# Two transformer blocks on one core: adaptive-norm blocks moved out of the even attention, its bias added by VectorE, its constants awaited later

## The reference

```python
def adaln(cond, w, b):                       # six shifts, scales and gates per layer, from the condition
    m = jax.nn.silu(cond) @ w + b            # 1024 -> 6144
    return jnp.split(m[:, None, :], 6, axis=-1)

# layer 0, the even mixer: 8 heads of window attention with a sink, 8 of neighbourhood attention
s_loc = jnp.einsum('bnqgrd,bnkgd->bngrqk', qb, kb) * scale
s_loc = jnp.where(valid[None, :, None, None], s_loc, NEG_INF)          # window: a mask
p = jax.nn.softmax(jnp.concatenate([s_loc, s_ctx, s_sink], axis=-1), axis=-1)
...
s_loc = jnp.einsum('brqhd,brikhd->brhqik', qg, kg) * scale + bias[None]   # near: a learned bias
s_loc = jnp.where(col_ok[:, None, :], s_loc, NEG_INF)
p = jax.nn.softmax(jnp.concatenate([s_loc, s_ctx], axis=-1), axis=-1)
```

## Time and profile before

| | |
|---|---|
| runs | 1917.2, 1918.7, 1922.2 us; median 1918.7 |
| profiled execution | 1921.6 us, span 1919.7 us |
| mean granted TensorE clock | 0.963 |
| TensorE busy | 1783.1 us, 93% of the span |
| VectorE, ScalarE, GpSimd busy | 927.3, 631.1, 183.8 us |
| bytes moved | 253.9 MB, mean 132 GB/s |

### The profile page before, as it was taken

The page is one execution under the profiler, slowest core; times in us unless marked ns, Lnnn a source line. Parts: engine busy times, 40 slices in busy tenths (PEclk is TensorE's granted clock), DMA queues, the critical chain, the costliest instruction groups (busy, mean ns, idle before and its releaser), DMA issues.

```text
span 1919.7 us, 25440 instructions
## 1 busy us (share of the span) xinstructions
PE 1783.1 (93%) x10056; PEld 1342.9 (70%) x10056; DVE 927.3 (48%) x1639; ACT 631.1 (33%) x1183; POOL 183.8 (10%) x202
## 2 busy tenths in 40 slices
PE   4999999989999999898989999899889789989998
PEld 1444555458888887453679998566679679879997
DVE  2122655254343433355736664434569853545544
ACT  3111544132222232233625443313322144034443
POOL 1001000100000001033000001001149200000000
PEclk8999999989999999998999999799889989999999
DMA  9222998132222321222044443223110234334442
GB/s 378 76 88 88 385 367 345 44 131 88 88 88 93 122 93 58 76 83 88 1 173 175 177 176 137 84 108 123 51 71 1 88 132 176 116 148 176 162 152 83
DMA packets 20885, 253.88 MB, mean 132 GB/s; under 512 B 2208, under 2 KB 4512, under 8 KB 5024
## 3 DMA queue, kind: packets, MB, share of 16 engines
q1 hardware_dynamic: 17712, 242.44, 33.2%
q10 hardware_dynamic: 3056, 9.82, 1.4%
HBM read 251.20 MB, written 1.05 MB: 131 GB/s over the span
## 4 chain that ended last, share of the span: by engine, by line
PE 81%; DVE 6%; POOL 4%; ACT 3%; issue 3%; DMA 2%; DVEq 0%; POOLq 0%; SPq 0%; ACTq 0%
PE bank L489 26%; PE bank L515 13%; PE bank L516 13%; PE bank L517 13%; PE bank L573 3%; PE bank L647 3%; PE bank L675 2%; POOL slab L2042 2%; PE bank L660 2%; PE bank L904 2%; DVE w_lo L1538 1%; POOL slab L2028 1%; DMA weights<-in_ada 1%; PE bank L652 1%; ACT w_hi L1147 1%
## 5 line engine op out<-in xcount | busy, mean ns | idle before, releaser
L489 PE MATMUL bank<-slab,weights 128*128 128x256 f32 (+2 forms) x1456 | 450.9, 469 | 17.5 <-DMA consts<-in_c 10.1
L489 PEld LDWEIGHTS bank<-slab,weights 128*128 128x128 f32 (+1 forms) x1456 | 277.7, 192 | 184.1 <-issue 141.0
L1538 DVE TENSOR_TENSOR w_lo<-weights,w_hi 128x1024 fp32r<-128x1024 f32 (+1 forms) x220 | 264.4, 1212 | 95.6 <-ACT w_hi L1147 94.8
L515 PE MATMUL bank<-h_hi,w_hi 128*128 128x256 f32 (+1 forms) x864 | 278.3, 322 | 25.4 <-DVE h_lo L1559 15.1
L1147 ACT ACTIVATE w_hi<-weights 128x1024 fp32r<-128x1024 f32 (+1 forms) x220 | 228.5, 1047 | 214.2 <-PE bank L517 209.5
L516 PE MATMUL bank<-h_lo,w_hi 128*128 128x256 f32 (+1 forms) x864 | 277.0, 321 | 0.0
L517 PE MATMUL bank<-h_hi,w_lo 128*128 128x256 f32 (+1 forms) x864 | 275.5, 319 | 0.0
L515 PEld LDWEIGHTS bank<-h_hi,w_hi 128*128 128x128 f32 x864 | 166.0, 192 | 42.2 <-issue 29.5
L516 PE MATMUL bank<-mlp_hidden_lo,w_hi 128*128 128x512 f32 (+1 forms) x512 | 174.4, 341 | 0.0
L516 PEld LDWEIGHTS bank<-h_lo,w_hi 128*128 128x128 f32 x864 | 166.2, 192 | 11.3
L517 PEld LDWEIGHTS bank<-h_hi,w_lo 128*128 128x128 f32 x864 | 165.6, 192 | 12.0
(11 more groups left out here) (206 smaller groups left out, 2338.4 us busy)
## 6 DMA issues: line engine op xcount, KB each, us to landing
weights<-in_ada SPq DMA_DIRECT2D x36, 2048.0 KB, 8.6
weights<-in_mlp_up SPq DMA_DIRECT2D x16, 2048.0 KB, 8.3
weights<-in_mlp_down SPq DMA_DIRECT2D x16, 2048.0 KB, 8.4
weights<-in_ffn_in SPq DMA_DIRECT2D x11, 2048.0 KB, 7.5
weights<-in_in SPq DMA_DIRECT2D x8, 2048.0 KB, 8.4
weights<-in_gate SPq DMA_DIRECT2D x6, 2048.0 KB, 7.5
weights<-in_ffn_out SPq DMA_DIRECT2D x8, 1408.0 KB, 6.0
weights<-in_even_in SPq DMA_DIRECT2D x4, 2048.0 KB, 11.6
```

Of the source, the lines that this page charges most:

```text
L489: last = mm(b[rows, 0:width], lhsT(k), rhs(k), start=k == 0, stop=k == kc - 1)
L515: mm(b[:, 0:width], wh, hi(k), start=k == 0, stop=False)
L1538: V.tensor_tensor(split_part(w_lo, q), raw_part(q), split_part(w_hi, q).bitcast(F32), ALU.subtract)\
```

## The change

1. *The table of adaptive-norm blocks.* The even attention keeps 18 of its 25 blocks, in four steps of seven (`7 * j // 4`). The other seven go: one behind the norm `mix1`, one before the sums of squares of `cq`, one before `uq` item 3, one behind the rotation of `kr`, one before the value products, one after the second token tile of them, and one in the delta network before its fifth masked sum. A batch may now hold blocks of two layers; the batches end elsewhere, and fold 3 moves from the even attention to step 2 of the odd one.
2. *The bias.* TensorE no longer multiplies the identity by the bias in 32 units. VectorE takes the maximum over the 256 context columns, and one instruction adds the bias to the first 256 columns in the bank and takes the maximum of the result and of the first maximum. TensorE's wait for `near_ready` is gone.
3. *The constants.* TensorE waits for `c0_in` at item 4 of the first projection instead of before it.
4. *Ring slots.* Where a block now falls between the taking of a weight block and its end, the entry of that weight block is kept aside and set later.

```diff
@@ -398,12 +398,14 @@
         }
 
 
-        ADA_BATCHES = [(0, 0, 4), (0, 4, 12), (1, 0, 12), (2, 0, 5), (2, 5, 12)]
-        ADA_ORDER = [(batch, n, blk) for batch, (n, lo, hi) in enumerate(ADA_BATCHES) for blk in range(lo, hi)]
-        ADA_ENDS = [sum(hi - lo for _, lo, hi in ADA_BATCHES[:batch + 1]) for batch in range(len(ADA_BATCHES))]
-        ADA_START, ADA_ATT = 4, 25
-        ada_steps = [5 * j // 4 for j in range(ADA_ATT)]
-        ada_ended = {ada_steps[ADA_ENDS[batch] - ADA_START - 1]: batch for batch in (1, 2, 3)}
+        ADA_BATCHES = [[(0, 0, 4)], [(0, 4, 12)], [(1, 0, 10)], [(1, 10, 12), (2, 0, 6)], [(2, 6, 12)]]
+        ADA_ORDER = [(batch, n, blk) for batch, runs in enumerate(ADA_BATCHES)
+                     for n, lo, hi in runs for blk in range(lo, hi)]
+        ADA_SIZES = [sum(hi - lo for _, lo, hi in runs) for runs in ADA_BATCHES]
+        ADA_ENDS = [sum(ADA_SIZES[:batch + 1]) for batch in range(len(ADA_BATCHES))]
+        ADA_START, ADA_ATT = 4, 18
+        ada_steps = [7 * j // 4 for j in range(ADA_ATT)]
+        ada_ended = {"even": {ada_steps[ADA_ENDS[batch] - ADA_START - 1]: batch for batch in (1, 2)}, "odd": {0: 3}}
 
 
         def even_items():
@@ -560,18 +562,18 @@
             def ada_block():
 
                 batch, n, blk = ADA_ORDER[ada[0]]
-                _, lo, hi = ADA_BATCHES[batch]
-                row = SIDES * (blk - lo)
+                at = ada[0] - ADA_ENDS[batch] + ADA_SIZES[batch]
+                row = SIDES * at
                 w = take_block(f"ada{n}", blk)
                 if ada[0] == 0:
                     pe.wait_ge(sem("cond_ready"), 2)
-                if blk == lo and batch:
+                if at == 0 and batch:
                     pe.wait_ge(sem("ada_copied"), batch)
                 window = slice(ADA_WIDE - SIDES - row, 2 * ADA_WIDE - SIDES - row)
                 for k in range(DC):
                     strip = slice(k % 4 * ADA_WIDE, (k % 4 + 1) * ADA_WIDE)
                     ins = mm(banks[ADA_BANK][strip, :], cond[:, n // 2, k, window], w[:, k, :],
-                             start=blk == lo and k < 4, stop=blk == hi - 1 and k >= 4)
+                             start=at == 0 and k < 4, stop=at == ADA_SIZES[batch] - 1 and k >= 4)
                 ins.then_inc(sem("ada_used"), 1)
                 ada[0] += 1
                 stream[-1][2] = ("ada_used", ada[0])
@@ -644,12 +646,7 @@
                         tags = [(name, "s", 2 * p), (name, "s", 2 * p + 1)]
                         for u, t in zip(pair, tags):
                             b = open_group(t)
-                            ins = mm(b[:, 0:u["n"]], u["q"], u["k"], start=True, stop=u["bias"] is None)
-                            if u["bias"] is None:
-                                close(ins, t)
-                        for u, t in zip(pair, tags):
-                            if u["bias"] is not None:
-                                close(mm(bank(t)[:, 0:LAT], ident, u["bias"], start=False, stop=True), t)
+                            close(mm(b[:, 0:u["n"]], u["q"], u["k"], start=True, stop=True), t)
                     if lag <= p < n + lag:
                         for j in (2 * (p - lag), 2 * (p - lag) + 1):
                             u = units[j]
@@ -679,8 +676,8 @@
                                     ins.then_inc(sem(f"{name}_pv"), 1)
                     if name == "even" and p in ada_steps:
                         ada_block()
-                    if name == "even" and p - 2 in ada_ended:
-                        ada_fold(ada_ended[p - 2])
+                    if p - 2 in ada_ended[name]:
+                        ada_fold(ada_ended[name][p - 2])
 
             def h_ready(name):
                 return lambda k: pe.wait_ge(sem(f"{name}_h"), k + 1)
@@ -712,7 +709,6 @@
             for _ in range(ADA_START - 2):
                 ada_block()
             ada_fold(0)
-            pe.wait_ge(sem("c0_in"), 16)
             items = ITEMS["even"]
             for blk in range(3):
                 w = take_block("even_in", blk)
@@ -722,6 +718,8 @@
                             before=h_ready("mix0") if i == 0 else None)
                     if mi == 3:
                         release_block(("even", i))
+                    if i == 4:
+                        pe.wait_ge(sem("c0_in"), 16)
                     if i and i % 4 == 0:
                         means_of("even", i // 4 - 1)
                     if i % 4 == 1 and i > 4:
@@ -745,7 +743,6 @@
             release_block(("vb", 3))
             rope("even", 4)
             pe.wait_ge(sem("even_roped"), 5)
-            pe.wait_ge(sem("near_ready"), 1)
             for t in range(4):
                 drained(pe, ("va", t))
                 drained(pe, ("vb", t))
@@ -757,6 +754,7 @@
 
 
             norm("mix1", TOK)
+            ada_block()
             pe.wait_ge(sem("c1_in"), 16)
             w = take_block("odd_in", 0)
             for i in range(3):
@@ -766,6 +764,8 @@
             release_block(("ckv", 0))
             w = take_block("odd_in_b", 0)
             product(("ckv", 1), DC, lambda k: w[:, k, 0:P], lambda k: h[:, k, :])
+            in_b = stream[-1]
+            ada_block()
             for name, n, width in (("cq", 3, LAT), ("ckv", 2, TOK)):
                 t = (name, "ss")
                 b = open_group(t, which=n)
@@ -776,17 +776,20 @@
                         ins.then_inc(sem(f"{name}_used"), 1)
                 close(ins, t)
             product(("kr", 0), DC, lambda k: w[:, k, P:P + 32], lambda k: h[:, k, :], rows=slice(64, 96))
-            release_block(("kr", 0))
+            in_b[2] = ("kr", 0)
             mean_of("kr", 0)
             pe.wait_ge(sem("cq_scaled"), 3)
             for blk in range(2):
                 w = take_block("uq", blk)
+                entry = stream[-1]
                 for hi in range(8):
                     i = blk * 8 + hi
+                    if i == 3:
+                        ada_block()
                     product(("uq", i), 3, lambda k: w[:, k, hi * MLA_QK:(hi + 1) * MLA_QK], lambda k: cq[:, k, :],
                             rows=slice(0, MLA_QK), width=LAT)
                     if hi == 7:
-                        release_block(("uq", i))
+                        entry[2] = ("uq", i)
                     if i and i % 4 == 0:
                         means_of("uq", i // 4 - 1)
                     if i >= 7 and i % 4 == 3:
@@ -814,15 +818,19 @@
             rope("uq", 15)
             release_block(("uk", 7))
             w = take_block("ukv", 1)
+            entry = stream[-1]
+            ada_block()
             for t in range(4):
                 for half in range(2):
                     product(("uv", 2 * t + half), 2, lambda k: ckv[:, k, t * P:(t + 1) * P],
                             lambda k: w[:, k, half * 512:(half + 1) * 512])
                 if t == 0:
                     means_of("uk", 1)
+                if t == 1:
+                    ada_block()
                 if t >= 2:
                     spread_of("uk", 1, 2 * (t - 2), 2)
-            release_block(("uv", 7))
+            entry[2] = ("uv", 7)
             pe.wait_ge(sem("uq_roped"), MLA_HEADS)
             pe.wait_ge(sem("uk_scaled"), 8)
             pe.wait_ge(sem("kr_copied"), MLA_HEADS)
@@ -928,6 +936,8 @@
                         heads(("qk", t), lambda hd: kT[:, hd, t * P:(t + 1) * P],
                               lambda hd: qT[:, hd, t * P:(t + 1) * P], which=1)
                 branch(*((6, "sx") if n < 4 else (4, "sb")), n % 4)
+                if n == 3:
+                    ada_block()
             tokens_first("kt", kT, "k_unit")
             for li in range(len(LEVELS)):
                 for t in range(4):
@@ -1190,8 +1200,8 @@
                 lag = a["lag"]
                 nprob, nprobT = len(a["prob"]), len(a["probT"])
                 for i in range(n + lag + 1):
-                    if name == "even" and i % 2 == 0 and i // 2 - 1 in ada_ended:
-                        ada_copy(ada_ended[i // 2 - 1])
+                    if i % 2 == 0 and i // 2 - 1 in ada_ended[name]:
+                        ada_copy(ada_ended[name][i // 2 - 1])
                     if i < n:
                         u = units[i]
                         t = (name, "s", i)
@@ -1404,14 +1414,17 @@
 
             def ada_bias(batch):
 
-                n, lo, hi = ADA_BATCHES[batch]
                 t = ("adaT", batch)
                 filled(dve, t)
-                got = bank(t)[:, 0:4 * ADA_WIDE].rearrange("p (m b s) -> p b m s", m=4, s=SIDES)[:, 0:hi - lo, :, :]
-                at = slice(4 * lo, 4 * hi)
-                V.tensor_tensor(mod[n][:, at, :].rearrange("p (b m) s -> p b m s", m=4), got,
-                                par(f"ada_b{n}").rearrange("p (b m s) -> p b m s", m=4, s=SIDES)[:, lo:hi, :, :], ALU.add)\
-                    .then_inc(free(t), 1)
+                got = bank(t)[:, 0:4 * ADA_WIDE].rearrange("p (m b s) -> p b m s", m=4, s=SIDES)
+                at = 0
```

(24 more changed lines are left out.)

## The result

The changed kernel takes **1910.2 us** (median of 6 runs, 1905.9 to 1912.3) against 1920.5 us for the kernel before in the same rounds (6 runs, 1917.2 to 1922.2): a ratio of 0.9945, 95% interval 0.9929 to 0.9961. It is faster, by 10.3 us. I had forecast 1897 us and a range that ended at 1906: half of the forecast gain is missing. A second measurement of the same kernel, beside a median of 1919.9 us for the kernel before, gave 1908.7 us (0.9938, 0.9918 to 0.9958).

The account below looks back on a forecast made before the run. TensorE was taken as the bound nearly everywhere. The terms -8.2 - 17.0 - 14.0 + 6.5 + 10.9 = -21.8 us gave 1899.8 us for the profiled execution, 1897 us as median; range 1888 to 1906 us.

Parts of the forecast that it names:

- part 4: Even attention: TensorE waits for VectorE in steps without a block and in heads with sinks, +6.5 us (+3 to +14).
- Part 1: Start: even constants awaited at item 4, first product at 34.14 us instead of 42.37, -8.2 us.
- Rival E: Start: bound otherwise, the even constants not the last to come, so little gained there; 1905 us, chance 0.03.
- Part 2: Even attention: bias by VectorE takes 17.0 us off TensorE; VectorE pays +0.25 us a unit (+0.15 to +0.55).
- rival A: Even attention: VectorE's adding instruction costs double, +0.55 us a unit; time 1904 to 1905 us, chance 0.12.
- Part 2 and 3: Even attention: TensorE loses 16 pairs of bias products, -17.0 us, and seven blocks and one fold, -14.0 us.
- Rival C: Even attention: the clock falls after waits of 1.5 to 1.8 us, three falls of 1.7 us; 1902 us, chance 0.1.
- Part 5: Six blocks to odd projections, one to delta network, a fold to odd attention: +10.9 us, including +5.2 at uq item 3.
- Rival B: Odd projections: the ring starves the scattered blocks, each later one waiting for its load; +10 us, 1907 us, chance 0.06.
- Rival D: Even attention: VectorE becomes the bound if the adding instruction takes some 1.6 us; about 1931 us at 1.8, chance 0.03.

Follow-up runs that it names:

- aligned: The changed kernel with the same 18 even-attention blocks put in the 16 steps that carry a bias, and steps 2 and 30: 1894.1 us (0.9856).
- after_again: The changed kernel itself, unchanged, measured again in later rounds: 1908.7 us (0.9938).
- blocks_only: The kernel before with only the new list of blocks; bias still on TensorE, constants awaited at the old place: 1917.9 us (0.9983).
- mixed: The changed kernel with TensorE adding the bias again in the six steps that carry a bias but no block: 1901.2 us (0.9899).
- bias_left_out: The changed kernel with no bias added to the even scores, VectorE taking one maximum over 512 columns as before: 1897.6 us (0.9879).
- bias_only: The kernel before with only the bias moved to VectorE; the old 25 blocks stay in the even attention: 1912.0 us (0.9948).
- gaps: The changed kernel with blocks as in `aligned`, query-projection block at item 7, and two more odd-projection blocks moved into TensorE waits: 1891.8 us (0.9849).

## Why the prediction was wrong

The step that failed is part 4, the waits of the even attention: a cover that was not there, and the clock that such waits cost, which the sum had at nothing. The stage took 134.6 us, above the 132 that were named as the sign of being wrong. The start and the rest held.

- **Part 1**, the constants: forecast -8.2, measured -7.45. Right; h's first chunk became the bound at 34.92 instead of 34.14. Rival E falls.
- **Part 2**, the adding instruction: forecast +0.25 a unit between +0.15 and +0.55, measured +0.31 (0.493 us for the addition, 0.142 for the read-out, against 0.43 and 0.15). Right, and rival A falls. The Trainium skill, Vector Engine (DVE) Microarchitecture Reference, Points that are easy to get wrong, has the rate halved for two SBUF sources that are not bf16. Here one source is in a bank, and 256 columns took 0.493 us, which is in keeping with it; no run has both sources in SBUF, so the halving itself is not shown.
- **Part 2 and 3**, what leaves TensorE: forecast -31.0. Take out of each stage its idle and what the clock cost: before 149.5 - 2.6 - 3.1 = 143.8; aligned, which has after's instructions, 118.9 - 4.0 = 114.9. So -28.9: the bias pairs were worth 0.92 us rather than 1.06, since the first transposes had run within their 1.06. An error of 2.1.
- **Part 4 failed.** "Together 9.1, of which 2.6 are there already: +6.5 us." Measured in after: 134.6 - 114.9 = 19.7 us beside the work, of which 6.8 by the clock and 12.9 in waits. So waits rose by 10.3 and the clock cost 3.7 more, +14.0 for +6.5. The latency in it was nearly right (4.0 us forecast, 4.2 measured), and so was its end, the Exp. Wrong was the cover. I had set "0.53 + 0.44 + 1.02 + 1.06", as if one half of a pair's scores lay between the first unit's end and the transposes: without the bias products both scores end together, so that 0.53 is no cover. Six steps of 0.53 make 3.2 us, and the six steps without a block do take 10.7 us in the rows where I had 7.4. That the rows show 9.7 us of idle, close to my 9.1, is luck: part of the loss stands as busy time, in seven pairs of scores whose second product had to wait for its bank. Three are rows of 1.68 to 1.74 us instead of 1.13, four are two rows of 0.70 instead of one, 4.5 us in all. (The remainder 12.9 - 9.7 = 3.2 is smaller, in part because the 6.8 us of the clock, summed over windows, hold waits too.) What had been meant as the bound, +14 at +0.55 a unit, came at +0.31.
- **Rival C**, the clock in the even attention, came true at chance 0.1: two falls, one of 1.7 us as I had given it and one of 3.4 (the windows from 213.3 to 225.3 and from 231.3 to 243.3); the first window, 1.7 us against 3.0 before, took 1.4 of these 5.1 back. I had treated it as an alternative to the forecast, when it was a consequence of it: "1.03 did not lower it, 1.35 did elsewhere" stood in my own text beside forecast waits of 1.5 to 1.8 us. Waits and clock had to be in the sum together.
- **Part 5**: +10.9, of which +9.6 in the odd projections, where I measure +11.2. The wait at item 3 was forecast as 2.0 and 1.3 for the clock and measured as 3.05 and 1.4 (a block of 3.33 instead of 1.92). In aligned and after_again it was the same, 3.1 us with a fall behind; in blocks_only, mixed and bias_left_out it was 1.64 to 1.85, with no fall. From the issue of its load to its first product it took 8.8 us here (793.93 to 802.73) and 7.6 in blocks_only; why it is one or the other is open. The gap before the values is gone, as forecast, and the delta network's idle went from 4.32 to 2.15 us, with the block in front.
- Rival B (the ring starves) is refuted for the attention by bias_only, and it is what gaps ran into elsewhere. Rival D never came near: VectorE is busy 94 of 134.5 us.

The sum: 2.1 (work) + 3.8 (waits) + 3.7 (clock) = 9.6 us, the whole of what the even attention lacked. Of the waits' 3.8, 3.2 are the false cover. The warning stood in the earlier trace rows: a step without a block waited already, with the old units and the old score pairs.

## What to carry to other kernels

When work is taken from a bounding engine and given to one that it waits for, ask step by step which work still covers the latency, and what each wait ends on, here a bank and not the input; then place the movable work where the latency is longest. Here that order of 18 blocks, one line, was worth some 15 us, more than the change itself. A wait on TensorE can carry the clock's price with it, and belongs in the sum with it, but its length alone does not decide it. In the even attention falls came with waits of 1.35 us and with one of 1.03 (bias_left_out), not with others of 1.03 or 1.09, and in the odd projections 1.64 to 1.85 us passed without a fall. And moving one load in a ring shifts the slot of every load behind it.

## What the runs showed that I had not expected

- Adding 5.5 us of products to TensorE made a stage 4.5 us shorter than in after_again, 5.6 than in after (mixed), as the granted clock stayed at 1.00 instead of 0.96 and 0.95.
- Busy time can hold a loss: a pair of scores runs side by side in 0.70 us, but when the second product has to wait for its bank each takes 0.70 of its own, and the idle column shows only the 0.35 us between them. A long row, on the other hand, can be the clock alone: eight transposes took 1.94 us instead of 1.06 at a granted clock of 0.50.
- 9 us less work on VectorE, at 70% busy, shortened the stage by 7.7 us against after_again (bias_left_out), and one line of order got 14.6 us with none of VectorE's work gone (aligned).
- A block's flight of 7.4 to 8.8 us cost 1.64 to 3.07, 0 or 5.47 us of waiting, by how long before its use its slot was freed.
